# A hybrid decoder layer on one core: eight projections by seven products of quarter blocks, with sums of weight blocks on GpSimd

## The chip, the cores and the metric

The kernel runs on one NeuronCore of one Trainium2 chip, written directly against the engines: TensorE (PE) for products, VectorE (DVE), ScalarE (ACT) and GpSimd (POOL) for the rest, SyncE (SP) for most DMAs. Each engine works off its own list in order and waits on semaphores. The metric is the device time of one launch in microseconds (us). All data is float32.

## The reference

One layer on 256 tokens of width 2048 (batch 1). In short:

```
mod = silu(c) @ ada_w + ada_b                  # 2048 x 12288, split into six parts of 2048
h   = rms(x, g1) * (1 + sc1) + sh1
z   = h @ w_in                                 # 19 column groups of up to 512: m_*, b_*, r_*, n_*
y   = concat(mlstm(m_*), moba(b_*), retention(r_*), nsa(n_*))     # 4 heads of 128 each
x   = x + gate1 * (y @ w_out)
h2  = rms(x, g2) * (1 + sc2) + sh2
x   = x + gate2 * moe(h2)                      # 32 experts of width 512, top 2 of 8 in the top group
```

`nsa` also compresses its keys and values: windows of 32 tokens, flattened to 4096 values, go through a 4096x128 matrix (`cmp_w1`), GELU and a 128x128 matrix.

## The kernel before

**Layout.** The normalised tokens lie transposed in `hT` (128 partitions x 16 k-tiles x 256 tokens). The weights come as a stream of 88 "halves" of 2 MB (128 x 4096 floats, eight k-tiles of 512 columns) through a ring of four SBUF slots, `ring`, in the order of `STREAM`. SP issues the DMA of half i as soon as half i-4 has been used; who used it is known from `halves_used`. Two halves make a "chunk": the projection of one column group, called `chunk` in the code, 2048x512 weights.

**Stages.** (1) The start: eight steps that compute the first adaLN parts from halves shared by PE and DVE, and beside it three projections from rows that come by another path (`early`). (2) The list `ORDER`, which all engines walk through in step: chunks, steps of the four mixers, and `ada` steps. An `ada` step is 1/24 of the adaLN product, two halves, done wholly on DVE: a `tensor_scalar` and 15 `scalar_tensor_tensor` of 128x512, each adding weight tile times scalar to `ada_s`. PE then sums `ada_s` over partitions (`ada_combine`, the step `ada_sum`, right after the next chunk). (3) `y @ w_out` in four column blocks, with the router's products between. (4) The expert loop: 8 passes over 4 experts, 24 halves each, through eight slots of 2 MB, four of them ring slots.

**A chunk.** For a plain chunk PE multiplies each 128x128 tile of `hT` (stationary) with 512 columns of weights (moving): 32 matmuls into two PSUM banks of `W`, line 575. `m_q`, `m_k`, `r_q`, `r_k` are made transposed, 64 matmuls of 256 columns with weights stationary, line 567. ACT copies the result to SBUF in one instruction (line 1031). Consecutive chunks use different halves of `W`. DVE has nothing to do with a chunk. In a trace each float32 matmul stands as two records.

**Around it.** The compression (`cmp_hid`, line 636) runs 64 matmuls with a 128x128 weight tile stationary and 60 columns of windows moving. GpSimd takes square roots for norms (`rsqrt`, line 428, 128x8), issues a few DMAs, and clears a buffer before the experts (line 477); its list follows `ORDER` too. Sums of the g2 part of adaLN (`ada` steps 20 to 23) go through PE into `A`, and DVE adds them to `g2b`.

## Time and profile before

| | |
|---|---|
| median of 3 runs | 1763.21 us (1759.32 to 1765.27) |
| the profiled execution | 1761.94 us, its span 1759.4 us |
| busy | PE 1395.3 us (79%), PE weight loads 886.8 us, DVE 549.9 us, ACT 126.9 us, POOL 27.3 us |
| DMA | 613.18 MB, 349 GB/s on average |

The page of the profile gives for each engine its busy time; a line of 40 digits is the span in 40 slices of 44 us, busy share in tenths. Stage 1 ends at about 138 us, stage 2 at about 683 us, stage 3 at about 804 us, and the rest is the expert loop.

### The profile page before, as it was taken

The page shows a single profiled execution, that of the slowest core. Times are in us where ns is not written, and L with a number is a line of the kernel's source. Part 1 is how long each engine was busy: PE and PEld are TensorE (multiplying, and loading weights), DVE is VectorE, ACT ScalarE, POOL GpSimd, SP SyncE. Part 2 cuts the span into 40 slices and gives each one's busy share as a digit, 9 for nine tenths or more (in the row PEclk, how much of TensorE's full clock was granted, in tenths as well). Part 3 has the DMA queues.
Part 4 walks back from the last instruction along what each step waited for, and adds up shares of the span by engine and source line. Part 5 has one row for each costly group of instructions (what it writes and reads, how often), then busy time and mean ns, then how long its engine had stood idle before and what let it go on. Part 6 is the DMA issues. An engine that isn't in the chain of part 4 may idle for free.

```text
span 1759.4 us, 28215 instructions
## 1 busy us (share of the span) xinstructions
PE 1395.3 (79%) x12793; PEld 886.8 (50%) x12793; DVE 549.9 (31%) x902; ACT 126.9 (7%) x279; POOL 27.3 (2%) x30
## 2 busy tenths in 40 slices
PE   6998999999998998998677766776666666566757
PEld 4664755865444865467454443534443535344434
DVE  3545443754537343302212112121211120121203
ACT  2001010101000100002000000000000000000000
POOL 0000000000001000001000000000000000000000
PEclk9999799999999999998988788877887888788878
DMA  9997475766674584655999999999999999999995
GB/s 404 426 427 314 156 307 210 284 237 255 252 278 189 236 318 172 245 232 232 408 426 427 428 427 427 427 427 427 427 427 428 427 428 427 427 428 427 427 428 243
DMA packets 44615, 613.18 MB, mean 349 GB/s; under 512 B 4896, under 2 KB 5168, under 8 KB 6736
## 3 DMA queue, kind: packets, MB, share of 16 engines
q1 hardware_dynamic: 42848, 604.00, 83.0%
q0 software_dynamic: 1072, 6.44, 0.9%
q8 instruction: 109, 1.79, 0.4%
q10 hardware_dynamic: 576, 0.87, 0.1%
q14 instruction: 10, 0.08, 0.0%
HBM read 609.19 MB, written 2.10 MB: 347 GB/s over the span
## 4 chain that ended last, share of the span: by engine, by line
DMA 49%; PE 42%; DVE 6%; issue 1%; ACT 1%; POOL 0%; SPq 0%; DVEq 0%
DMA Zpad<-in_exp_w 34%; PE W L575 14%; DMA ring<-in_stream 8%; DMA ring<-in_exp_w 6%; PE M L939 5%; PE W L859 5%; PE W L567 3%; DVE ada_s L1230 3%; PE A L963 2%; PE W L913 2%; PE W L900 2%; PE W L841 2%; PE M L636 1%; PE M L551 1%; DVE tmp L1174 1%
## 5 line engine op out<-in xcount | busy, mean ns | idle before, releaser
L575 PE MATMUL W<-ring,buf_h 128*128 128x512 f32 x704 | 309.3, 600 | 4.2 <-DMA ring<-in_stream 4.1
L1230 DVE SCALAR_TENSOR_TENSOR ada_s<-ring,small,ada_s 128x512 f32<-128x512 f32 x296 | 222.6, 752 | 10.5
L575 PEld LDWEIGHTS W<-ring,buf_h 128*128 128x128 f32 x704 | 134.8, 193 | 171.6 <-issue 171.6
L939 PE MATMUL M<-ring,g1b 128*32 128x128 f32 x4096 | 153.5, 308 | 82.8 <-DMA ring<-in_exp_w 70.7
L939 PE MATMUL M<-Zpad,g1b 128*32 128x128 f32 x3072 | 129.1, 340 | 84.1 <-DMA Zpad<-in_exp_w 56.9
L939 PEld LDWEIGHTS M<-ring,g1b 128*32 128x32 f32 x4096 | 131.3, 124 | 115.8 <-DMA ring<-in_exp_w 93.8
L939 PEld LDWEIGHTS M<-Zpad,g1b 128*32 128x32 f32 x3072 | 113.1, 139 | 104.8 <-DMA Zpad<-in_exp_w 63.7
L1687 DVE SCALAR_TENSOR_TENSOR tmp<-tmp,M 128x128 f32<-128x128 f32 x32 | 9.2, 288 | 474.3 <-ACT tmp L1152 474.3
L1174 DVE TENSOR_TENSOR consts<-A,g2b 32x512 f32<-32x512 f32 x128 | 87.9, 687 | 213.7 <-PE A L963 210.7
L567 PE MATMUL W<-buf_h,ring 128*128 128x256 f32 x512 | 112.9, 383 | 11.1 <-DMA ring<-in_stream 11.1
L567 PEld LDWEIGHTS W<-buf_h,ring 128*128 128x128 f32 x512 | 98.1, 192 | 24.9 <-issue 11.5
L963 PE MATMUL A<-ring,tmp 128*32 128x512 f32 x512 | 80.0, 767 | 28.5 <-DMA ring<-in_exp_w 24.5
L963 PE MATMUL A<-Zpad,tmp 128*32 128x512 f32 x384 | 63.8, 795 | 37.5 <-DMA Zpad<-in_exp_w 34.3
L913 PE MATMUL W<-consts,tmp 128*128 128x512 f32 x128 | 72.0, 715 | 19.1 <-DVE buf_h L1174 19.1
L859 PE MATMUL W<-ring,buf_x 128*128 128x512 f32 x192 | 83.2, 593 | 1.2 <-ACT buf_x L1098 1.2
L900 PEld LDWEIGHTS W<-tmp,buf_x 128*128 128x128 f32 x576 | 70.2, 204 | 13.3 <-issue 13.2
L900 PE MATMUL W<-tmp,buf_x 128*128 128x128 f32 x576 | 71.9, 289 | 0.0
L1152 ACT ACTIVATE tmp<-M 128x128 f32<-128x128 f32 x32 | 8.9, 277 | 756.6 <-PE M L939 756.6
L1174 DVE TENSOR_TENSOR buf_h<-W,buf_h 128x2048 f32<-128x2048 f32 (+1 forms) x20 | 39.4, 1970 | 64.9 <-PE W L913 64.6
L541 PE MATMUL W<-buf_h,Zpad 128*128 128x256 f32 x256 | 58.3, 387 | 1.3 <-DVE buf_h L1255 1.3
L859 PEld LDWEIGHTS W<-ring,buf_x 128*128 128x128 f32 x192 | 36.2, 190 | 45.5 <-issue 44.0
L913 PEld LDWEIGHTS W<-consts,tmp 128*128 128x128 f32 x128 | 27.6, 226 | 58.6 <-issue 32.9
(285 smaller groups left out, 937.3 us busy)
## 6 DMA issues: line engine op xcount, KB each, us to landing
ring<-in_exp_w SPq DMA_DIRECT2D x96, 2048.0 KB, 35.6
ring<-in_stream SPq DMA_DIRECT2D x88, 2048.0 KB, 8.6
Zpad<-in_exp_w SPq DMA_DIRECT2D x72, 2048.0 KB, 36.6
PPY<-in_exp_w SPq DMA_DIRECT2D x24, 2048.0 KB, 35.5
Zpad<-in_early SPq DMA_DIRECT2D x8, 1536.0 KB, 10.6
buf_x<-in_x SPq DMA_DIRECT2D x2, 1024.0 KB, 6.7
buf_h<-in_x POOLq DMA_DIRECT2D x1, 2048.0 KB, 12.2
out<-buf_h SPq DMA_DIRECT2D x4, 512.0 KB, 3.1
```

Of the source, the lines that this page charges most:

```text
L541: ins = pe.matmul(dst[:, h * T:h * T + T], w[:, first + 512 * k + h * P:first + 512 * k + h * P + P], hT[:, kk, :], start=(kk == 0 and h % ...
L551: ins = pe.matmul(dst[:, tt * 512:tt * 512 + 512], hT[:, kk, tt * P:tt * P + P], w[:, first + 512 * k:first + 512 * k + 512], start=(kk == ...
L567: ins = pe.matmul(dst[:, h * T:h * T + T], w[:, 512 * k + h * P:512 * k + h * P + P], hT[:, kk, :], start=(kk == 0 and h % 2 == 0), stop=( ...
L575: ins = pe.matmul(dst[:, tt * 512:tt * 512 + 512], hT[:, kk, tt * P:tt * P + P], w[:, 512 * k:512 * k + 512], start=(kk == 0), stop=(kk == ...
L841: ins = pe.matmul(W[:, p0:p0 + 256], YT[:, kk, tt * P:tt * P + P], w[:, p1:p1 + 256], start=(kk == 0 and tt == 0), stop=(kk == KT - 1), sk ...
L859: ins = pe.matmul(W[:, o + tt * 512:o + tt * 512 + 512], YT[:, kk, tt * P:tt * P + P], w[:, 512 * k:512 * k + 512], start=(kk == 0), stop= ...
L900: ins = pe.matmul(W[:, k * P:k * P + P], xs[:, tt, k * P:k * P + P], tmp[:, 128 * tt:128 * tt + 128], start=(tt == 0), stop=(tt == 1))
L913: ins = pe.matmul(W[:, 512 * b:512 * b + 512], GT[:, tt * P:tt * P + P], ysb[:, 512 * b:512 * b + 512], start=True, stop=True)
L939: ins = pe.matmul(M[32 * c:32 * c + 32, 512 * w13:512 * w13 + 128], XT[:, kk, 32 * q:32 * q + 32], w[:, 512 * k + 128 * c:512 * k + 128 * ...
L963: ins = pe.matmul(A[32 * m:32 * m + 32, :], hTs[:, 32 * c:32 * c + 32], w[:, 2048 * c2 + 512 * m:2048 * c2 + 512 * m + 512], start=(c == 0 ...
L1174: return dve.tensor_tensor(o, x, y, op)
L1230: ins = dve.scalar_tensor_tensor(acc[:], w, cs[:, kk:kk + 1], acc[:], ALU.mult, ALU.add)
```

## The change

**Seven products.** For the eight chunks of `SEVEN`, weights and tokens are cut in quarters: `A11..A22` are 128-token by 8-k-tile quarters of `hT`, `B11, B12` the two column halves of the first weight half, `B21, B22` those of the second. Instead of eight quarter products there are seven, of sums and differences (the form of Strassen and Winograd). Each product is 8 matmuls of 256 columns into one bank of `W`; all four banks are used. DVE makes the four token sums `S1..S4` once, in `buf_x`. GpSimd makes four weight sums for each chunk, in place in the ring slots (`column_sums`), each a `tensor_tensor` of 128 x 2048. Two products are copied by ACT into the output, and DVE adds the rest in seven short operations (`add_quarters`), which stand in DVE's list where `ORDER` has the chunk, so behind the `ada` step ahead of it. Both halves of such a chunk are released only when the sixth or seventh product and all four weight sums are done.

**The rest.** The ring has five slots. In the last part of `ORDER` the `ada` steps 19 to 22 stand right behind their chunk. `cmp_hid` has the windows stationary (64 columns) and 128 weight columns moving, in two column groups of the array; a copy and two small matmuls then add the two groups. The four g2 `ada` steps accumulate in `g2b` itself; one set of four 512-column matmuls sums it over partitions while the router is worked out, and ACT copies it back. A few waits of the router's exponentials on DVE come later. The expert loop keeps its eight slots.

```diff
-         ('chunk', 'b_q'), ('m_pv', 0), ('norm', 'b_q'), ('ada', 19),
-         ('chunk', 'b_k'), ('turn', 'b_q'), ('turn_y', 'm'), ('norm', 'b_k'), ('ada', 20),
-         ('chunk', 'r_q'), ('turn', 'b_k'), ('scores', 'moba'), ('ada', 21),
-         ('chunk', 'r_k'), ('turn_p', 'moba'), ('ada', 22),
+         ('chunk', 'b_q'), ('ada', 19), ('m_pv', 0), ('norm', 'b_q'),
+         ('chunk', 'b_k'), ('ada', 20), ('turn', 'b_q'), ('turn_y', 'm'), ('norm', 'b_k'),
+         ('chunk', 'r_q'), ('ada', 21), ('turn', 'b_k'), ('scores', 'moba'),
+         ('chunk', 'r_k'), ('ada', 22), ('turn_p', 'moba'),
...
+                    of_kind, of_arg, of_hf = STREAM[i - RING]
                     if by_vector(STREAM[i - RING]):
                         sp.wait_ge(sem["ada_half_used"], dve_halves)
+                    elif of_kind == 'chunk' and of_arg in SEVEN:
+                        sp.wait_ge(sem["products_done"], 7 * SEVEN.index(of_arg) + 6 + of_hf)
+                        sp.wait_ge(sem["t_ready"], 4 * SEVEN.index(of_arg) + 4)
...
+            def column_sums(name):
+
+                n, _ = sevens(name)
+                (w0, full0, fills0), (w1, full1, fills1) = chunk_slots(name)
+                b11, b12, b21, b22 = side(w0, 0), side(w0, 1), side(w1, 0), side(w1, 1)
+                pool.wait_ge(full0, fills0)
+                pool.wait_ge(sem["products_done"], 7 * n + 1)
+                pool.tensor_tensor(b11, b12, b11, ALU.subtract).then_inc(sem["t_ready"], 1)
+                pool.wait_ge(sem["t_ready"], 4 * n + 1)
+                pool.wait_ge(full1, fills1)
+                pool.tensor_tensor(b12, b22, b12, ALU.subtract).then_inc(sem["t_ready"], 1)
+                pool.wait_ge(sem["products_done"], 7 * n + 3)
+                pool.wait_ge(sem["t_ready"], 4 * n + 2)
+                pool.tensor_tensor(b11, b22, b11, ALU.subtract).then_inc(sem["t_ready"], 1)
+                pool.wait_ge(sem["t_ready"], 4 * n + 3)
+                pool.tensor_tensor(b21, b21, b11, ALU.subtract).then_inc(sem["t_ready"], 1)
+
             for step, arg in ORDER:
-                if step == 'cmp_out':
+                if step == 'chunk' and arg in SEVEN:
...
+            def seven_products(name):
+
+                n, c = sevens(name)
+                (w0, full0, fills0), (w1, full1, fills1) = chunk_slots(name)
+                after_seven = CHUNKS[c - 1] in SEVEN
+
+                def product(i, left, w, col):
+                    b = i % 4 * 512
+                    for k in range(8):
+                        ins = pe.matmul(W[:, b:b + 256], left[:, k, :], w[:, 512 * k + 256 * col:512 * k + 256 * col + 256],
+                                        start=(k == 0), stop=(k == 7))
+                    ins.then_inc(sem["products_done"], 1)
+                    return ins
+
+                if after_seven:
+                    pe.wait_ge(sem["quarter_added"], 6 * n - 2)
+                else:
+                    pe.wait_ge(sem["chunk_copied"], 2 if n == 0 else c - 1)
+                pe.wait_ge(full0, fills0)
+                product(0, A11, w0, 0)
+                if after_seven:
+                    pe.wait_ge(sem["quarter_added"], 6 * n)
+                pe.wait_ge(full1, fills1)
+                product(1, A12, w1, 0)
+                pe.wait_ge(sem["t_ready"], 4 * n + 1)
+                if n == 0:
+                    pe.wait_ge(sem["s_ready"], 4)
+                else:
+                    pe.wait_ge(sem["chunk_copied"], c)
+                product(2, S1, w0, 0)
+                product(3, S4, w1, 1)
+                pe.wait_ge(sem["t_ready"], 4 * n + 2)
+                pe.wait_ge(sem["quarter_kept"], 2 * n + 1)
+                product(4, S3, w0, 1)
+                pe.wait_ge(sem["t_ready"], 4 * n + 3)
+                pe.wait_ge(sem["quarter_added"], 6 * n + 1)
+                product(5, S2, w0, 0)
+                pe.wait_ge(sem["t_ready"], 4 * n + 4)
+                pe.wait_ge(sem["quarter_kept"], 2 * n + 2)
+                product(6, A22, w1, 0)
+                half[0] += 2
...
                         pe.wait_ge(sem["blocks_ready"], w + 1)
                         for l in range(CMP_LEN):
-                            ins = pe.matmul(M[:, 512 * w:512 * w + 60], wt[:, l * P:l * P + P],
-                                            blk[w][:, l * 60:l * 60 + 60], start=(l == 0), stop=(l == CMP_LEN - 1))
+                            o = l % 2 * 64
+                            ins = pe.matmul(M[o:o + 64, 512 * w:512 * w + P], blk[w][:, l * 60:l * 60 + 64],
+                                            wt[:, l * P:l * P + P], start=(l < 2), stop=(l >= CMP_LEN - 2))
                         half_done(ins)
+                    pe.wait_ge(sem["hid_parts"], 1)
+                    for w in range(2):
+                        ins = pe.matmul(M[:, 1280 + 64 * w:1344 + 64 * w], hpart[:, w * P:w * P + P], const('selr'),
+                                        start=True, stop=True)
+                    ins.then_inc(sem["hid_summed"], 1)
...
+            def add_quarters(name):
+
+                n, c = sevens(name)
+                z = zslot[name]
+                z11, z12, z21, z22 = (z[:, 256 * i:256 * i + 256] for i in range(4))
+                right = z.rearrange("p (a h) -> p a h", a=TT)[:, :, 256:512]
+                second = z[:, 512:1024].rearrange("p (c h) -> p c h", c=2)
+
+                def twice(v):
+                    return v.unsqueeze(1).to_broadcast([P, 2, 256])
+
+                dve.wait_ge(sem["quarter_kept"], 2 * n + 1)
+                dve.wait_ge(sem["products_done"], 7 * n + 2)
+                tt_op(z11, W[:, 512:768], z21, ALU.add).then_inc(sem["quarter_added"], 1)
+                dve.wait_ge(sem["quarter_kept"], 2 * n + 2)
+                dve.wait_ge(sem["products_done"], 7 * n + 4)
+                tt_op(z12, W[:, 1536:1792], z22, ALU.add).then_inc(sem["quarter_added"], 1)
+                dve.wait_ge(sem["quarter_added"], 6 * n + 2)
+                tt_op(right, right, twice(z21), ALU.add).then_inc(sem["quarter_added"], 1)
+                dve.wait_ge(sem["quarter_added"], 6 * n + 3)
+                dve.wait_ge(sem["products_done"], 7 * n + 5)
+                tt_op(second, second, twice(W[:, 0:256]), ALU.add).then_inc(sem["quarter_added"], 1)
+                dve.wait_ge(sem["quarter_added"], 6 * n + 4)
+                dve.wait_ge(sem["products_done"], 7 * n + 6)
+                tt_op(z12, z12, W[:, 512:768], ALU.add).then_inc(sem["quarter_added"], 1)
+                tt_op(second, second, twice(W[:, 512:768]), ALU.add).then_inc(sem["quarter_added"], 1)
+                dve.wait_ge(sem["quarter_added"], 6 * n + 6)
+                dve.wait_ge(sem["products_done"], 7 * n + 7)
+                dve.wait_ge(sem["chunk_copied"], c)
+                tt_op(z21, z21, W[:, 1024:1280], ALU.add).then_inc(sem["chunk_copied"], 1)
+
```

On PE, in stage 2, the chunk `n_ks` stood before as two pieces, each waiting for its half (`slot_full`), followed by the sum of the `ada` step:

```order
L575 MATMUL W<-ring,buf_h 128x512 [waits slot_full2,chunk_copied]
L575 MATMUL W<-ring,buf_h 128x512 x15
L575 MATMUL W<-ring,buf_h 128x512 [waits slot_full3]
L575 MATMUL W<-ring,buf_h 128x512 x15
L532 MATMUL A<-consts,ada_s 128x1 [waits ada_combined,ada_half_used]
L532 MATMUL A<-consts,ada_s 128x1 x3
```

In the changed kernel the same place on PE reads (`t_ready` counts GpSimd's weight sums, `quarter_kept` ACT's copies, `quarter_added` DVE's additions):

```order
L610 MATMUL W<-ring,buf_h 128x256 [waits slot_full3,chunk_copied]
L610 MATMUL W<-ring,buf_h 128x256 x7
L610 MATMUL W<-ring,buf_h 128x256 [waits slot_full4]
L610 MATMUL W<-ring,buf_h 128x256 x7
L610 MATMUL W<-ring,buf_x 128x256 [waits s_ready,t_ready]
L610 MATMUL W<-ring,buf_x 128x256 x15
L610 MATMUL W<-ring,buf_x 128x256 [waits quarter_kept,t_ready]
L610 MATMUL W<-ring,buf_x 128x256 x7
L610 MATMUL W<-ring,buf_x 128x256 [waits quarter_added,t_ready]
L610 MATMUL W<-ring,buf_x 128x256 x7
L610 MATMUL W<-ring,buf_h 128x256 [waits quarter_kept,t_ready]
L610 MATMUL W<-ring,buf_h 128x256 x7
```

32 matmuls of 512 columns have become 56 of 256, and PE now waits inside the chunk for three other engines: the third product for the first weight sum, the sixth for DVE's first addition.

On GpSimd, the changed kernel's list around the chunks `n_vs` and `n_kw` is this (L454 is the square root, L475 to L483 the weight sums; before, only the three L454 rows, as L428, stood here):

```order
L454 TENSOR_TENSOR small<-small 128x8 [waits norm_ms]
L475 TENSOR_TENSOR ring<-ring 128x8x256 [waits products_done,slot_full4]
L478 TENSOR_TENSOR ring<-ring 128x8x256 [waits slot_full0,t_ready]
L481 TENSOR_TENSOR ring<-ring 128x8x256 [waits t_ready,products_done]
L483 TENSOR_TENSOR ring<-ring 128x8x256 [waits t_ready]
L454 TENSOR_TENSOR small<-small 60x1 [waits kc_ms]
L454 TENSOR_TENSOR small<-small 128x8 [waits norm_ms]
L475 TENSOR_TENSOR ring<-ring 128x8x256 [waits products_done,slot_full3]
L478 TENSOR_TENSOR ring<-ring 128x8x256 [waits slot_full4,t_ready]
L481 TENSOR_TENSOR ring<-ring 128x8x256 [waits t_ready,products_done]
L483 TENSOR_TENSOR ring<-ring 128x8x256 [waits t_ready]
```

So the weight sums of `n_vs` stand behind the square root of the norm of `n_q`, and those of `n_kw` behind that of `n_ks`.

On DVE, ahead of the additions of `m_v`, the changed kernel has the `ada` step 14 (L1345, L1347) and then the convolution of `m_k` (L1618 to L1629):

```order
L1345 TENSOR_SCALAR ada_s<-ring,small 128x512 [waits slot_full2,dve_step]
L1347 SCALAR_TENSOR_TENSOR ada_s<-ring,small,ada_s 128x512 [waits dve_step] x7
L1347 SCALAR_TENSOR_TENSOR ada_s<-ring,small,ada_s 128x512 [waits slot_full3,ada_half_used]
L1347 SCALAR_TENSOR_TENSOR ada_s<-ring,small,ada_s 128x512 [waits dve_step] x7
L1618 TENSOR_SCALAR Zpad<-Zpad,cols 128x256 [waits chunk_copied,ada_half_used]
L1618 TENSOR_SCALAR Zpad<-Zpad,cols 128x256 x3
...
L1293 TENSOR_SCALAR tmp<-tmp 128x1024 [waits conv_tanh]
L1629 SCALAR_TENSOR_TENSOR Zpad<-Zpad,tmp 128x1024 [waits dve_step]
L1286 TENSOR_TENSOR Zpad<-W,Zpad 128x256 [waits products_done,quarter_kept] x2
L1286 TENSOR_TENSOR Zpad<-Zpad 128x2x256 [waits quarter_added]
L1286 TENSOR_TENSOR Zpad<-Zpad,W 128x512 [waits products_done,quarter_added]
```

Before, the same work stood there without the last three rows; now the products of `m_v` past the fifth need it to be finished.

## Rows read from the trace of the kernel before

**Rows 1.** Stages: us, busy of PE, PEld, DVE, ACT, POOL, clock, DMA share, GB/s.

```profile
138.00:683.00 545.00, 516.19 (x1818) 320.53 (x1819) 264.97 (x401) 51.27 (x90) 13.85 (x12) 0.95 0.65 250
171.00:197.00 26.00, 25.66 (x129) 25.66 (x130) 4.22 (x12) 3.40 (x4) 0.00 (x0) 0.55 0.36 138
860.00:1740.00 880.00, 588.78 (x9307) 383.26 (x9296) 156.52 (x269) 39.59 (x126) 0.00 (x0) 0.82 1.00 424
```

**Rows 2.** Timeline of PE: start, us, instruction, idle before and its releaser.

```profile
138.31 29.40 PE L575 MATMUL W<-ring,buf_h 128*128 128x512 f32 x64 [3.75 <-DMA ring<-in_stream]
196.67 29.79 PE L575 MATMUL W<-ring,buf_h 128*128 128x512 f32 x64
...
230.55 27.70 PE L575 MATMUL W<-ring,buf_h 128*128 128x512 f32 x64
...
338.48 27.86 PE L567 MATMUL W<-buf_h,ring 128*128 128x256 f32 x128 [2.35 <-DMA ring<-in_stream]
...
369.75 27.63 PE L575 MATMUL W<-ring,buf_h 128*128 128x512 f32 x64
...
400.73 27.63 PE L575 MATMUL W<-ring,buf_h 128*128 128x512 f32 x64
...
573.10 29.47 PE L567 MATMUL W<-buf_h,ring 128*128 128x256 f32 x128 [8.71 <-DMA ring<-in_stream]
...
608.23 27.79 PE L567 MATMUL W<-buf_h,ring 128*128 128x256 f32 x128
...
770.51 1.08 PE L808 MATMUL A<-Zpad,consts 128*64 128x256 f32 x8
```

**Rows 3.** Page, costliest groups: busy us, mean ns of one.

```profile
L575 PE MATMUL W<-ring,buf_h 128*128 128x512 f32 x704 | 309.3, 600 | 4.2 <-DMA ring<-in_stream 4.1
```

**Rows 4.** Groups by line and shape: busy us, mean ns of one.

```profile
L1174 DVE TENSOR_TENSOR buf_h<-W,buf_h 128x2048 f32<-128x2048 f32 x16 | 36.7, 2291 | 64.6 <-PE W L913 64.6
...
L477 POOL MEMSET consts<- 32x2048 f32 x4 | 7.2, 1796 | 0.7 <-PE M L817 0.4
```

**Rows 5.** Timeline of POOL.

```profile
201.81 1.67 POOL L428 TENSOR_TENSOR small<-small 128x8 f32<-128x8 f32 x1 [78.02 <-DVE small L1177]
...
233.38 1.65 POOL L428 TENSOR_TENSOR small<-small 128x8 f32<-128x8 f32 x1 [2.98 <-DVE small L1177]
...
537.58 2.03 POOL L428 TENSOR_TENSOR small<-small 128x8 f32<-128x8 f32 x1 [135.81 <-DVE small L1177]
...
687.08 2.03 POOL L428 TENSOR_TENSOR small<-small 128x8 f32<-128x8 f32 x1 [11.56 <-DVE small L1177]
...
806.02 7.54 POOL L477 MEMSET consts<- 32x2048 f32 x4 [0.39 <-PE M L817]
```

**Rows 6.** Timeline of DVE in stage 2, with the `ada` steps 9 and 15.

```profile
204.66 0.48 DVE L1228 TENSOR_SCALAR ada_s<-ring,small 128x512 f32<-128x512 f32 x1
205.18 11.78 DVE L1230 SCALAR_TENSOR_TENSOR ada_s<-ring,small,ada_s 128x512 f32<-128x512 f32 x15
...
384.87 1.14 DVE L1454 TENSOR_SCALAR Zpad<-Zpad,cols 128x256 f32<-128x256 f32 x4
...
392.99 1.23 DVE L1465 SCALAR_TENSOR_TENSOR Zpad<-Zpad,tmp 128x1024 f32<-128x1024 f32 x1
...
405.42 11.78 DVE L1230 SCALAR_TENSOR_TENSOR ada_s<-ring,small,ada_s 128x512 f32<-128x512 f32 x15
```

**Rows 7.** Timeline of DVE beside three of POOL's pieces of rows 5.

```profile
537.39 0.69 DVE L1181 TENSOR_SCALAR Zpad<-Zpad 128x1024 f32<-128x1024 f32 x1
...
687.62 1.22 DVE L1174 TENSOR_TENSOR PPY<-PPY,Zpad 128x1024 f32<-128x1024 f32 x1
...
812.67 0.92 DVE L1626 TENSOR_SCALAR small<-small 128x8 f32<-128x8 f32 x1
```

**Rows 8.** Timeline of PE: a sum of an `ada` step; the wait in the router.

```profile
602.41 1.02 PE L529 MATMUL A<-ada_s,consts 128*128 128x512 f32 x2
...
810.90 0.69 PE L888 MATMUL M<-tmp,consts 128*128 128x64 f32 x2 [5.04 <-DVE tmp L1174]
```

More of the change, by code:

```diff
@@ L101 @@
 MIXED = 'nmbr'
+SEVEN = ('n_ks', 'n_vs', 'n_kw', 'n_vw', 'm_v', 'm_o', 'b_v', 'r_v')
 MIX_Y = {'m': 0, 'b': 1, 'r': 2, 'n': 3}
@@ L125 @@
 STREAM = weight_stream()
-RING = 4
+RING = 5
 HALF = 8 * 512
@@ L139, in halves_used @@
     v = sum(by_vector(STREAM[j]) for j in range(i))
-    return i - v, v
-FIRST_FILLS = EXPERT_BASE // RING
+    seven = sum(STREAM[j][0] == 'chunk' and STREAM[j][1] in SEVEN for j in range(i))
+    return i - v - seven, v
+FIRST_FILLS = [len(range(i, EXPERT_BASE, RING)) for i in range(RING)]
 EXPERT_RING = 8
@@ L608, in _ @@
                     ada_combine(arg)
+                elif step == 'chunk' and arg in SEVEN:
+                    seven_products(arg)
                 elif step == 'chunk':
@@ L1284, in _ @@
             for step, arg in ORDER:
-                if step == 'ada':
+                if step == 'chunk' and arg in SEVEN:
+                    add_quarters(arg)
+                elif step == 'ada':
                     ada_accumulate(arg)
```

186 lines of the change are left out of this document (118 added, 68 removed).

## The prediction

> **What bounds the kernel now.** I read the stages first. In the expert loop the DMA engines are busy all the time at 424 GB/s while PE is busy for 589 of 880 us; in stage 2 PE is busy for 516 of 545 us and the DMA engines for 65% of it [rows 1]. So from 138 to about 804 us PE's list sets the pace, and after that the transfers, whose number does not change. A microsecond taken out of PE's path ahead of the experts starts that train of transfers a microsecond earlier, and so comes off the end; one taken out of PE in the loop would be worth nothing. Everything below is therefore a sum over PE's time in stages 2 and 3.
>
> Then PE's timeline. A chunk takes 27.6 us (the row at 400.73); the first takes 29.4, the one behind the compression 29.8, both with an idle or slow stretch just ahead of them [rows 2]. Over its 11 chunks the line is busy for 309.3 us [rows 3], 28.1 each, so the eight that change cost 225 us. The compression fills the stretch from 171 to 197 us, at a mean granted clock of 0.55, near the lower level of 1.2 GHz, although PE is busy for 25.7 of 26 us in it [rows 1]. Three more places matter: waits of 2.35 and 8.71 us for ring halves, the second followed by a chunk of 29.5 us where its like takes 27.8 [rows 2].
>
> **The change, part by part.** *Products.* 64 matmuls of 256 columns take 27.79 us [rows 2], so a product of 8 takes p = 3.47 us. Seven take 24.3 us against 27.6, if PE never waits. But it does wait. The first weight sum can start when product 1 is done, at 3.47 us, and product 3 needs it. With s for one sum, product 3 starts at 3.47 + s, and five products follow: the chunk takes 20.8 + s by this path, and 6.9 + 4s by GpSimd's own chain, which the last product closes.
>
> *What s is.* The trace has no such operation on GpSimd. Its one pass over 2048 elements, a memset, takes 1.80 us [rows 4]; a sum makes two reads and a write. If these ran wholly beside each other, s would be 1.8 us; one after another, 5.4 us. DVE's nearest operation takes 2.29 us [rows 4]. GpSimd is a programmed engine (a square root of 8 elements takes 1.67 us [rows 5]), so I take the upper part: two and a half passes, 4.5 us. Then the chunk takes 25.3 us, 2.3 less than before. The bounds give 24.3 (s under 3.47) and 28.5 us. The Trainium skill (GPSIMD Engine Reference, "Performance versus the Vector engine") gives 4497 ns for such a float32 sum and says to leave elementwise work to the Vector engine; by it the chunk would come out at the same 25.3 us. No run shows it yet.
>
> *Where GpSimd comes late.* In its list the sums of `n_vs` stand behind the square root of the norm of `n_q`, which ended 6.8 us into that chunk (201.81 + 1.67 - 196.67), those of `n_kw` behind one that ended 4.5 us into theirs (233.38 + 1.65 - 230.55) [rows 2, 5]. These chunks become 6.8 + 4.5 + 5 x 3.47 = 28.7 and 26.3 us.
>
> *Where DVE comes late.* Product 6 needs DVE's first addition, and that stands behind an `ada` step. If DVE is free for it D us after the chunk's start, the chunk takes at least D + 0.45 + 2p = D + 7.4. From the trace of before D is 20.3 for `n_vs` (216.96 - 196.67), 16.3 for `m_o` (417.2 - 400.9) and 24.5 for `m_v`, with the convolution between (394.22 - 369.75) [rows 2, 6]; the other five lie between 12.7 and 18.0 and end in the same way. Only `m_v` is bound by it: 31.9 us. Sums so far: 27.6 for the first chunk (25.3, and 2 us as before for its start and for the second half, which lands 2.1 MB / 424 GB/s = 4.9 us after the first and is now needed at 3.5), 28.7, 26.3, 31.9 and four of 25.3: 215.7 us, 10 less than before.
>
> *What the two engines do to each other.* The trace shows one thing surely. A tiny `TENSOR_SCALAR` on DVE, of 8 elements, lasted 0.92 us and ended at 813.59, just when GpSimd's memsets ended (806.02 + 7.54 = 813.56) [rows 5, 7]. And a square root on GpSimd took 2.03 us instead of 1.67 both times that it began during a `TENSOR_SCALAR` of 1024 elements on DVE [rows 5, 7]. So one-input operations of DVE from and to SBUF and any GpSimd operation exclude each other, for the whole operation. Each `ada` step begins with one (0.48 us), and the convolution has four [rows 6]. Where it falls within a sum of up to 4.5 us, DVE is late by the rest: in `n_vs` by 3.3 us (8.0 against 11.3), in `n_kw` by 3.3, in `m_o` by 4.0 (4.0 against 8.0), in `m_v` by about 6 (from 15, through two sums). By D + 7.4 these become 31.0, 28.7, 27.7 and 38 us. The eight chunks then come to 229 us, 4 **more** than before: in my forecast the seven products save nothing.
>
> *Compression.* The nearest row to 64 stationary and 128 moving columns in two groups is line 808: 4 matmuls (8 records) of 256 columns in 1.08 us, with 64 [rows 2]. Half as wide, 64 matmuls take 64 x 0.13 = 8.3 us. A copy of 0.4 us, two small matmuls and the hops between add 1.2. Against 25.7 us that is **-16**; if the clock stays at its lower level, 17 + 1.2 us, so -7.5. I take the first, as wide matmuls ran at the upper level just ahead.
>
> *Ring and order.* With `ada` 19 behind chunk `b_q` DVE does it while it now idles, and half i waits for i-5: the waits of 8.71 and 2.35 us go, and 1.7 of slow start: **-12.8**. Nothing else is late next: a chunk's first half waits for an `ada` half that DVE drops at D, 10 us before the next chunk, and lands in about 5.
>
> *g2.* Four sums of 0.86 us leave PE's path; the four matmuls that take their place lie in a wait of 5.04 us [rows 8], and ACT's copy of 2 us ends about when the gather starts: **-3.2**. DVE's four token sums of 1024 elements, some 5 us, lie where it waits for PE at the end of stage 1. The memsets, semaphores and late exponentials cost nothing, as they lie beside PE's work; uncovered they would be under 1 us.
>
> Sum: 4 - 16 - 12.8 - 3.2 = **-28 us**. The profiled execution took 1761.9 us (span 1759.4), 1.3 under the median. 1761.9 - 28 = **1734 us**.
>
> **The rivals.** *B: the engines hardly touch each other.* Then the chunks give their 10 us: -10 - 32 = -42, so 1720 us. For it: the exclusion is shown only for one-input operations. With s at its lower bound the chunks could lose another 10: 1710.
>
> *C: operations with two SBUF inputs are excluded too* (all 15 `scalar_tensor_tensor` of an `ada` step). Then DVE and GpSimd take turns, one operation each: while four sums of 4.5 us run, DVE gets about four of its 0.75 us steps. D grows by 18, and every chunk becomes D + 25.4: from 38 to 50 us, 341 us for the eight, 116 more than before: 1761.9 + 116 - 32 = 1846 us. It decides from 4 us more in each chunk, where it eats up the other 32. For it: both would read through what the shorter ones fight for. Against it: the `TENSOR_TENSOR` at 687.62 had two inputs in SBUF, ran while GpSimd's square root ran (687.08 to 689.11), took its usual 1.22 us, and did not lengthen that one beyond 2.03 [rows 5, 7]; but that operation reads only 8 elements. The Trainium skill says so outright (SBUF — State Buffer, "SBUF: two separate sides"): DVE in a two-port mode, or with two SBUF inputs against a GpSimd operation that reads SBUF, and GpSimd hold an exclusive lock for the whole instruction. By that rule the result is C; the rows bear it out for the first kind only. If DVE keeps the lock until its `ada` step is through, the sums start at D instead, and it ends near 1800.
>
> *D: a wash.* s at 5.4 us or a partial exclusion puts 3 to 4 us more on each chunk, and gains and losses cancel: 1755 to 1770.
>
> **How the numbers follow.** Forecast (1722 to 1750): 0.38. B: 0.22. C: 0.32, as the mechanism is half shown. D: 0.08. Faster by over 0.3%: the first two and a quarter of D, 0.62. Within 0.3%, about what a measurement can tell here, half of D: 0.04. Slower: C and the rest, 0.34. The range from 1708 to 1846 leaves out the far half of C and little else; the forecast's own is 1720 to 1750.
>
> **What would show it.** The weight sums on GpSimd at 4.5 us; PE waiting in the sixth product of `n_vs`, `n_kw`, `m_o` and above all `m_v` for DVE; `TENSOR_SCALAR` of `ada` steps stretched to some us, but `SCALAR_TENSOR_TENSOR` at 0.75; the compression under 10 us with the clock above 0.9; no wait for the ring ahead of `r_q`; the expert loop as long as before. I would be wrong if `SCALAR_TENSOR_TENSOR` rows stretch beside GpSimd's sums or have gaps of their length (C), if the sums take over 5.5 us, if the compression runs at 1.2 GHz, or if halves of the ring, released late by chunks that hold both, make PE wait anew.

## The result, and the profile after

The changed kernel takes 1850.47 us (median of 4 runs, 1849.3 to 1851.36), the kernel before 1762.1 us in the same comparison (1759.32 to 1765.27). The ratio is 1.0501, with a 95% interval of 1.048 to 1.0521: 88 us slower, where I had forecast 28 us less, and 4.5 us outside my range. What happened is rival C, at 1846 us. The profiled execution has a span of 1849.2 us. Two of the kernels below had one execution each in a slower state, 1949 and 1964 us at a granted clock of 0.72 instead of 0.90; these two stand in the medians given, which they move by under 0.5 us, and in no ratio.

The stages first, with the columns of [rows 1]: all of stage 2, which now ends where the first product of `y @ w_out` starts, at 774.7 us; in it the compression; and the same piece of the expert loop, counted back from the end.

```profile
138.00:774.70 636.70, 487.90 (x2200) 385.19 (x2201) 426.25 (x456) 48.59 (x98) 166.83 (x44) 0.89 0.56 218
184.30:192.60 8.30, 7.71 (x133) 7.47 (x133) 4.29 (x12) 3.40 (x4) 0.00 (x0) 1.00 0.98 374
949.80:1829.80 880.00, 574.71 (x9288) 375.59 (x9280) 156.45 (x269) 39.56 (x126) 0.00 (x0) 0.84 1.00 423
```

The expert loop is what it was, at 423 GB/s with the DMA engines always busy. The compression is short and at the full clock, as forecast. The rest of stage 2 is another place: PE was busy for 516 of 545 us, now for 488 of 637, while DVE went up from 265 to 426 us and GpSimd from 14 to 167. PE does less and waits. For what, the list of PE's waits says (total us, times, longest):

```profile
PE W L610 <- DVE Zpad L1286: 92.0, 7, 15.7
...
PE W L610 <- ACT Zpad L1133: 23.7, 1, 23.7
```

Line 610 is the loop of the seven products. Seven of the eight chunks wait for DVE's additions, and `m_v` for a copy by ACT. The page's groups of DVE name the reason:

```profile
L1347 DVE SCALAR_TENSOR_TENSOR ada_s<-ring,small,ada_s 128x512 f32<-128x512 f32 x236 | 289.0, 1225 | 8.4
```

These 236 operations take 1225 ns on average, where the form took 752 before. Some of them lie in stage 1. The groups by line and shape from 138 to 810 us tell them apart from the others:

```profile
L1347 DVE SCALAR_TENSOR_TENSOR ada_s<-ring,small,ada_s 128x512 f32<-128x512 f32 x180 | 246.9, 1372 | 6.4
...
L1347 DVE SCALAR_TENSOR_TENSOR g2b<-ring,small,g2b 128x512 f32<-128x512 f32 x52 | 39.1, 751 | 1.7
L1286 DVE TENSOR_TENSOR Zpad<-Zpad,small 128x1024 f32<-128x1024 f32 x5 | 14.7, 2941 | 8.8 <-POOL small L454 8.8
L1345 DVE TENSOR_SCALAR ada_s<-ring,small 128x512 f32<-128x512 f32 x12 | 14.3, 1189 | 0.1
```

The steps into `g2b`, late in the stage, where no weight sum runs beside them, are at 751 ns; those into `ada_s`, 12 steps of which 8 stand beside sums, at a mean of 1372.

GpSimd's sums themselves are of the length that I took, 4.5 us alone. One chunk in full, `n_kw`, from the timelines of POOL, DVE and PE (start, us, instruction, idle before and its releaser):

```profile
247.45 4.49 POOL L475 TENSOR_TENSOR ring<-ring 128x2048 f32<-128x2048 f32 x1
252.02 5.38 POOL L478 TENSOR_TENSOR ring<-ring 128x2048 f32<-128x2048 f32 x1
257.55 4.51 POOL L481 TENSOR_TENSOR ring<-ring 128x2048 f32<-128x2048 f32 x1
262.14 4.82 POOL L483 TENSOR_TENSOR ring<-ring 128x2048 f32<-128x2048 f32 x1
```

```profile
247.51 5.52 DVE L1286 TENSOR_TENSOR Zpad<-Zpad,small 128x1024 f32<-128x1024 f32 x1 [1.76 <-POOL small L454]
252.95 4.74 DVE L1345 TENSOR_SCALAR ada_s<-ring,small 128x512 f32<-128x512 f32 x1
257.72 20.02 DVE L1347 SCALAR_TENSOR_TENSOR ada_s<-ring,small,ada_s 128x512 f32<-128x512 f32 x15
277.78 0.75 DVE L1286 TENSOR_TENSOR Zpad<-W,Zpad 128x256 f32<-128x256 f32 x2
```

```profile
242.70 7.07 PE L610 MATMUL W<-ring,buf_h 128*128 128x256 f32 x32
252.00 10.63 PE L610 MATMUL W<-ring,buf_x 128*128 128x256 f32 x48 [2.23 <-POOL ring L475]
278.35 6.75 PE L610 MATMUL W<-ring,buf_x 128*128 128x256 f32 x16 [15.73 <-DVE Zpad L1286]
284.94 3.62 PE L610 MATMUL W<-ring,buf_h 128*128 128x256 f32 x16
```

Read it across. A multiplication with two SBUF inputs, 1.22 us when alone, is issued 0.06 us behind the first sum and lasts 5.52 us: it waited until that sum was over, at 251.94, and ran. The second sum needed 0.9 us more than the first and the third, because it waited for that multiplication in turn. The `tensor_scalar` then sat out the second sum. The 15 steps of the `ada` took 20.02 instead of 11.78 us, 8.2 more, while two sums took 9.3: DVE got one operation in between each two sums and no more. PE has products 1 to 5 done at 262.63, 15.2 us before DVE comes to its first addition at 277.78.

Where only `scalar_tensor_tensor` stands beside all four sums, in the next chunk `n_vw`, the picture is purest (timelines of DVE, then POOL's first and last sum):

```profile
295.37 28.44 DVE L1347 SCALAR_TENSOR_TENSOR ada_s<-ring,small,ada_s 128x512 f32<-128x512 f32 x15
```

```profile
300.08 4.50 POOL L475 TENSOR_TENSOR ring<-ring 128x2048 f32<-128x2048 f32 x1 [33.12 <-PE W L610]
...
314.50 4.82 POOL L483 TENSOR_TENSOR ring<-ring 128x2048 f32<-128x2048 f32 x1
```

28.44 us instead of 11.78 is 16.7 more, and the four sums cover 19.2 us (300.08 to 319.32). The difference, 2.6 us, is about three steps of 0.75: the three operations let through between four sums. One step by itself, the one that begins while the second sum runs:

```profile
305.16 4.89 DVE L1347 SCALAR_TENSOR_TENSOR ada_s<-ring,small,ada_s 128x512 f32<-128x512 f32 x1
```

Its neighbours begin at 300.10, 310.08 and 315.00: one step for each sum, as long as the sum. From the second sum on each lasts 0.3 us longer than the 4.50 of the first; my reading is that it waits for the step that was let through.

So each chunk of seven products costs about D + 25.4 us, as rival C had it (D is where DVE was free before, from the start of the chunk, read from the timelines of the kernel before). The eight, from PE's timeline, start of the first product to the end of the last, against that formula:

| chunk | n_ks | n_vs | n_kw | n_vw | m_v | m_o | b_v | r_v | sum |
|---|---|---|---|---|---|---|---|---|---|
| D + 25.4 | 41.1 | 45.7 | 43.3 | 38.3 | 49.9 | 41.9 | 40.7 | 40.6 | 341 |
| measured | 41.7 | 46.3 | 45.9 | 39.3 | 52.5 | 42.1 | 41.1 | 41.2 | 350 |

The formula comes this close by two errors that offset each other. In the seven chunks other than `m_v` DVE reached its first addition 0.9 to 1.6 us earlier than D + 18, as three of its steps got through between the sums. And the last two products, for which it has 6.9 us, took 8.6 to 10.2, at granted clocks of 0.70 to 0.83 behind PE's wait of 9 to 16 us, 15 us over the seven chunks. In `n_kw`:

```profile
278.35:288.56 10.21, 10.21 (x35) 8.49 (x35) 2.58 (x5) 0.00 (x0) 0.00 (x0) 0.70 0.79 279
```

Against 226 us before the eight cost 124 us more, by the two timelines; the spans of the two profiled executions differ by 90; so all the rest of the change gave back about 34 us.

### The profile page after: what moved, and what is told of

Read it like the earlier page. It is cut to its first block, busy times and chain, and to the rows that moved or that the text cites. A ratio compares the mean times of both kernels' runs of the same rounds, so it can differ in the third digit from the quotient of the medians.

```text
span 1849.2 us, 29213 instructions
## 1 busy us (share of the span) xinstructions
PE 1354.3 (73%) x13181; PEld 942.2 (51%) x13181; DVE 715.4 (39%) x961; ACT 126.1 (7%) x288; POOL 180.3 (10%) x62
## 4 chain that ended last, share of the span: by engine, by line
DMA 44%; PE 36%; DVE 13%; issue 3%; POOL 1%; ACT 1%; SPq 0%; DVEq 0%; POOLq 0%
DMA Zpad<-in_exp_w 40%; DVE ada_s L1347 9%; PE W L657 6%; PE W L957 4%; PE W L665 4%; PE W L610 4%; PE M L1040 3%; PE W L587 2%; DMA ring<-in_exp_w 2%; PE A L1064 2%; PE W L939 2%; DMA ring<-in_stream 2%; PE M L597 1%; PE W L1013 1%; PE W L1000 1%
## 5 line engine op out<-in xcount | busy, mean ns | idle before, releaser
L1347 DVE SCALAR_TENSOR_TENSOR ada_s<-ring,small,ada_s 128x512 f32<-128x512 f32 x236 | 289.0, 1225 | 8.4
L1040 PE MATMUL M<-ring,g1b 128*32 128x128 f32 x4096 | 165.8, 329 | 102.5 <-DMA ring<-in_exp_w 97.3
L610 PE MATMUL W<-ring,buf_x 128*128 128x256 f32 x512 | 130.4, 419 | 128.7 <-DVE Zpad L1286 92.0
L1040 PEld LDWEIGHTS M<-ring,g1b 128*32 128x32 f32 x4096 | 143.7, 134 | 134.1 <-DMA ring<-in_exp_w 118.2
L610 PEld LDWEIGHTS W<-ring,buf_x 128*128 128x128 f32 x512 | 107.3, 213 | 151.7 <-issue 118.7
L1040 PE MATMUL M<-Zpad,g1b 128*32 128x128 f32 x3072 | 115.0, 306 | 73.1 <-DMA Zpad<-in_exp_w 41.3
L1040 PEld LDWEIGHTS M<-Zpad,g1b 128*32 128x32 f32 x3072 | 98.6, 123 | 95.2 <-DMA Zpad<-in_exp_w 47.6
L610 PE MATMUL W<-ring,buf_h 128*128 128x256 f32 x384 | 90.8, 394 | 5.3 <-DMA ring<-in_stream 5.3
L610 PEld LDWEIGHTS W<-ring,buf_h 128*128 128x128 f32 x384 | 75.6, 199 | 17.5 <-issue 5.6
L665 PE MATMUL W<-ring,buf_h 128*128 128x512 f32 x192 | 83.0, 593 | 0.0
```

The source lines that it names most:

```text
L610: ins = pe.matmul(W[:, b:b + 256], left[:, k, :], w[:, 512 * k + 256 * col:512 * k + 256 * col + 256], start=(k == 0), stop=(k == 7))
L665: ins = pe.matmul(dst[:, tt * 512:tt * 512 + 512], hT[:, kk, tt * P:tt * P + P], w[:, 512 * k:512 * k + 512], start=(kk == 0), stop=(kk == ...
L1040: ins = pe.matmul(M[32 * c:32 * c + 32, 512 * w13:512 * w13 + 128], XT[:, kk, 32 * q:32 * q + 32], w[:, 512 * k + 128 * c:512 * k + 128 * ...
L1347: ins = dve.scalar_tensor_tensor(acc, w, cs[:, kk:kk + 1], acc, ALU.mult, ALU.add)
```

## The experiments

The theory: a GpSimd operation that reads SBUF and a DVE operation with two inputs in SBUF exclude each other for whole instructions and take turns; the eight chunks are slow through that alone, and the rest of the change gains some 32 us. The rivals are named with each.

### Without seven products

All eight chunks in the plain form; ring, order, compression and g2 as changed. ACT's tanh of `m_o`, which stood with the seven products' copies, stands behind the plain copy.

```diff
-SEVEN = ('n_ks', 'n_vs', 'n_kw', 'n_vw', 'm_v', 'm_o', 'b_v', 'r_v')
+SEVEN = ()
```

> The changed kernel with no chunk done by seven products: all chunks as before (28 us each), the five ring slots, the order, the compression and the g2 sums as changed. Theory 1 (everything lost is lost in the eight chunks, by DVE and GpSimd taking turns): the other parts give their 32 us and a little more, as the compression's 64 matmuls took 7.4 us in the changed kernel's trace: 1728 us, 122 under the changed kernel. Rival (the five slots or the order themselves hurt, by transfers that come late): 1745 or more.

Measured: 1730.37 us, ratio 0.9792 (0.976 to 0.9825), and in a later comparison once more:

> The kernel without seven products again, on the same chip as old_ring_and_order: 1730 us, 2% under the kernel before.

Measured: 1731.57 us, ratio 0.98 (0.9773 to 0.9827). Here PE never waits for a chunk's weights but once, for 3.8 us, at the start of stage 2. The rest of the change is worth 33 us in this comparison and 30 in the later one, against the 32 of my sum, and this version beats both kernels. The eight seven-product chunks cost 120 us.

### What on GpSimd does the harm

Memsets in place of the weight sums, of the same total length: GpSimd is as busy and signals after about the same time, but reads nothing from SBUF.

```diff
-                pool.tensor_tensor(b11, b12, b11, ALU.subtract).then_inc(sem["t_ready"], 1)
+                fill(b11).then_inc(sem["t_ready"], 1)     # 2 memsets of 1.8 us, one of 0.95
... (the other three sums in the same way)
```

(The count of the expert rounds is set to one in this run and the next.)

> GpSimd's four sums of a chunk are replaced by memsets of the same region with about the same length (two of 1.8 us and one of 0.9, which read nothing); the weights of products 3 to 7 are thus constants, and the number of expert rounds is fixed at the one it has. Theory 1a (the exclusion is over the interface through which GpSimd and DVE's second input read): DVE's 15 additions of an ada step run at 0.75 us beside the memsets, only its one-input operations wait, at most 1.8 us: 1715 to 1735 us. Theory 1b (any GpSimd operation stops them): about 1850 us. Rival 2 (GpSimd's chain of four sums is what holds PE, not DVE): the chain is as long as before, so 1850 us too.

Measured: 1740.15 us, ratio 0.9871 (0.9855 to 0.9888). The groups of DVE and POOL by shape, stage 2:

```profile
L1356 DVE SCALAR_TENSOR_TENSOR ada_s<-ring,small,ada_s 128x512 f32<-128x512 f32 x180 | 135.3, 752 | 6.4
L1354 DVE TENSOR_SCALAR ada_s<-ring,small 128x512 f32<-128x512 f32 x12 | 7.7, 642 | 0.1
L1295 DVE TENSOR_TENSOR Zpad<-Zpad,small 128x1024 f32<-128x1024 f32 x5 | 6.1, 1224 | 8.8 <-POOL small L454 8.8
```

```profile
L473 POOL MEMSET ring<- 128x2048 f32 x64 | 116.1, 1814 | 126.4 <-PE W L619 122.9
```

With GpSimd busy as before but writing only, both two-input forms are back at 752 and 1224 ns. The one-input `TENSOR_SCALAR` is not: 642 ns, where it takes 480 with GpSimd idle. Those two classes of exclusion are thus told apart. It also refutes the rival by which GpSimd's chain of four holds PE whatever DVE does, at 1850 us. The upper end of the expectation, 1735, was 5 us too low: PE still waits 13.6 us for GpSimd and 12.9 once, in `m_v`, for ACT:

```profile
PE W L619 <- POOL ring L475: 13.6, 11, 3.1
PE W L619 <- ACT Zpad L1142: 12.9, 1, 12.9
```

So even where the engines hardly touch, the seven products cost 10 us over the kernel without them. Chunk by chunk on PE's timelines that is `m_v` alone: it takes 42.0 us, where the plain one takes 27.6; the other seven come to 197 us against 198. My rival B, 1720 us by a gain of 10 in the chunks, does not come out either, as it had `m_v` at 31.9.

### Which inputs on DVE do the harm

The weight sums as changed, but the `scalar_tensor_tensor` of the `ada` steps 8 to 17 reads its addend from PSUM (`A`), so that it has one input in SBUF.

```diff
-    ins = dve.scalar_tensor_tensor(acc, w, cs[:, kk:kk + 1], acc, ALU.mult, ALU.add)
+    ins = dve.scalar_tensor_tensor(acc, w, cs[:, kk:kk + 1],
+                                   A[:] if N_PAIRED <= n < 18 else acc, ALU.mult, ALU.add)
```

> GpSimd's sums stay. In the ada steps 8 to 17 the 15 additions read their addend from the PSUM tile A instead of SBUF, so they have one input in SBUF (their result is not the adaLN product then; the number of expert rounds is fixed at the one it has). Theory 1 (two SBUF inputs are what collides): the additions run beside the sums at 0.7 to 0.75 us; what still collides is the first operation of each step and the norms' products with two inputs, once in four chunks: 1730 to 1745 us. Rival (any DVE operation that reads SBUF is stopped, whatever its inputs): about 1850 us.

Measured: 1759.66 us, ratio 0.9977 (0.9965 to 0.9989). Groups of DVE and POOL by shape, stage 2:

```profile
L1347 DVE SCALAR_TENSOR_TENSOR ada_s<-ring,small,A 128x512 f32<-128x512 f32 x150 | 112.2, 748 | 5.3
L1286 DVE TENSOR_TENSOR Zpad<-Zpad,small 128x1024 f32<-128x1024 f32 x5 | 14.7, 2942 | 8.8 <-POOL small L454 8.8
L1345 DVE TENSOR_SCALAR ada_s<-ring,small 128x512 f32<-128x512 f32 x12 | 14.2, 1188 | 0.1
```

```profile
L475 POOL TENSOR_TENSOR ring<-ring 128x2048 f32<-128x2048 f32 x8 | 36.1, 4518 | 133.9 <-PE W L610 133.9
```

Beside the same sums the same operation takes 748 ns when one of its inputs comes from PSUM, and the first of the four sums takes 4.52 us on average. Nothing is left of the mutual wait but in the forms that this run did not touch: the norm's multiplication (2942 ns, with two inputs in SBUF) and the one-input `TENSOR_SCALAR` (1188 ns). They hold DVE up enough that PE still waits for it, 15.5 us in three chunks, and 13.9 in `m_v`. 91 of the 120 us are gone. The time is 15 us above the range that I expected, as I had named those forms and counted them too low, and had not counted `m_v`'s wait for ACT.

### DVE's first addition earlier

The first addition between the two halves of the `ada` step, in all chunks but `m_v`, so that product 6 does not wait for its second half.

```diff
+                ada_rows(n, 0, ...)
+                if n in after:
+                    add_first(after[n])
+                ada_rows(n, 1, ...)
```

> A correct kernel: DVE's first addition of a chunk, for which product 6 waits, stands between the two halves of the ada step instead of behind it (not in m_v, which has another step between). Theory 1 (turns of 4.5 us and 0.75 us): PE no longer waits in the chunk, but DVE's list is as long as before, 12 us of ada step and 18 us of GpSimd's sums one after another, and the next chunk's first product waits for DVE's fourth addition: 5 us less in seven chunks, about 1815 us. Rival (only the place of the addition in DVE's list was wrong): PE's wait of 9 to 16 us goes wholly, about 1750 us or less.

Measured: 1806.58 us, ratio 1.0243 (1.0226 to 1.026). PE's wait for DVE falls from 92.0 us to 32.9. A little over a third of the loss is gone, 44 of 120 us; the rest stays, as DVE loses as much in each chunk wherever the addition stands (the mean of its `ada_s` steps is 1389 ns), `m_v` still waits 23.7 us for ACT, and the waits for halves of the ring go up from 5.3 to 12.3 us.

### The same seven products with and without DVE's work beside them

Three chunks only, `m_o`, `b_v`, `r_v`; then the same with the `ada` steps 15, 16, 17 moved behind `r_v`, which shifts 18 and 19 too; then that move alone. (With plain chunks ahead of them, PE's first product in the two kernels with three waits for the copy of the chunk just ahead, not of the one before it.)

```diff
-SEVEN = ('n_ks', 'n_vs', 'n_kw', 'n_vw', 'm_v', 'm_o', 'b_v', 'r_v')
+SEVEN = ('m_o', 'b_v', 'r_v')
# the move
-         ('chunk', 'm_v'), ('scores', 'win'), ('ada', 15),
-         ('chunk', 'm_o'), ('turn_p', 'win'), ('pv', 'win'), ('ada', 16),
-         ('chunk', 'b_v'), ('m_decay', 0), ('ada', 17),
-         ('chunk', 'r_v'), ('turn_y', 'n'), ('m_scores', 0), ('ada', 18),
-         ('chunk', 'b_q'), ('ada', 19), ('m_pv', 0), ('norm', 'b_q'),
-         ('chunk', 'b_k'), ('ada', 20), ('turn', 'b_q'), ('turn_y', 'm'), ('norm', 'b_k'),
+         ('chunk', 'm_v'), ('scores', 'win'),
+         ('chunk', 'm_o'), ('turn_p', 'win'), ('pv', 'win'),
+         ('chunk', 'b_v'), ('m_decay', 0),
+         ('chunk', 'r_v'), ('turn_y', 'n'), ('m_scores', 0), ('ada', 15), ('ada', 16),
+         ('chunk', 'b_q'), ('ada', 17), ('m_pv', 0), ('norm', 'b_q'), ('ada', 18),
+         ('chunk', 'b_k'), ('ada', 19), ('turn', 'b_q'), ('turn_y', 'm'), ('norm', 'b_k'), ('ada', 20),
```

> The changed kernel with seven products in m_o, b_v and r_v only; the other five chunks take the plain form. Theory (turns): the DVE work that stands ahead of the first addition in these three (ada 15, 16, 17) is slowed by the four sums as in the changed kernel, where the three chunks took about 42, 41 and 41 us against 27.7: some 40 us over the kernel without seven products (1730), so about 1770 us, and SCALAR_TENSOR_TENSOR in these three ada steps at a mean of over 1.2 us, in the others at 0.75. Rival (the seven products cost by themselves, by hops and late halves of the ring, whatever DVE does beside them): also slower than 1730, but then by the same amount when the ada steps are moved away (the run three_sevens_ada_later).

> The same three chunks with seven products, but the ada steps 15, 16, 17 moved behind r_v, so that DVE has only short softmax and decay work beside the sums, and its first addition comes in time. Theory (turns): the loss of about 40 us goes nearly all; b_v and r_v come to 25 to 27 us each, m_o to about 28, and the kernel to 1725 to 1735 us, if moving the steps costs nothing by itself (see ada_later_alone). Rival (the form costs by itself): about 1770 us, as in three_sevens_beside_ada.

> No seven products, ada steps 15, 16, 17 behind r_v: what the move costs by itself. DVE was busy for 166 us of the 404 between 400 and 804 us in the kernel before, so there is room: 1730 us give or take 4, the same as the kernel without seven products. If the halves of the moved steps crowd the ring or the norms of b_q and b_k come late, up to 1750.

Measured: 1768.76 us (ratio 1.0024, 1.0002 to 1.0046), 1756.16 us (0.9951, 0.9928 to 0.9974), and 1758.44 us for the move alone (0.9954, 0.9932 to 0.9977). The first is on its expectation: 38 us over the kernel without seven products, 12.8 for each chunk. PE's timeline shows `b_v` in it, and behind it `b_v` in the second:

```profile
428.27 7.07 PE L610 MATMUL W<-ring,buf_h 128*128 128x256 f32 x32
436.95 10.63 PE L610 MATMUL W<-ring,buf_x 128*128 128x256 f32 x48 [1.61 <-POOL ring L475]
460.67 5.60 PE L610 MATMUL W<-ring,buf_x 128*128 128x256 f32 x16 [13.09 <-DVE Zpad L1285]
466.11 3.62 PE L610 MATMUL W<-ring,buf_h 128*128 128x256 f32 x16
```

```profile
414.52 7.07 PE L610 MATMUL W<-ring,buf_h 128*128 128x256 f32 x32
422.85 14.08 PE L610 MATMUL W<-ring,buf_x 128*128 128x256 f32 x64 [1.25 <-POOL ring L475]
437.01 3.72 PE L610 MATMUL W<-ring,buf_h 128*128 128x256 f32 x16
```

41.5 us (428.27 to 469.73) against 26.2 (414.52 to 440.73), with the same four sums on GpSimd in both. In the second, PE waits 3.8 us in all three chunks together, for GpSimd, and never for DVE. That refutes the rival by which the form costs by itself. It also shows what the form is worth at its best here: 1.4 us in `b_v`, where a plain chunk takes 27.6; `r_v`, at a lower clock for its first products, takes 28.0. Even there DVE's own two-input addition meets a sum (timeline of DVE, second kernel; 0.69 us alone):

```profile
430.58 2.00 DVE L1285 TENSOR_TENSOR Zpad<-Zpad 128x512 f32<-128x512 f32 x1
```

I was wrong on the move, which I had at 1730 us give or take 4. It costs 28 us by itself, and the list of PE's waits of that kernel says where:

```profile
PE W L665 <- DMA ring<-in_stream: 13.6, 3, 7.0
PE W L657 <- DMA ring<-in_stream: 9.9, 1, 9.9
```

DVE had the time, but halves are loaded in the stream's order, and those of the moved steps crowd where they now stand; my reading is that they hold the ring's slots until DVE, with two steps in a row, has used them. So the second kernel is to be compared with the third, not with 1730: it is 2 us faster, with ranges that overlap (1753.55 to 1759.15 us and 1750.88 to 1761.82 us). With DVE out of the way, seven products neither gain nor lose what can be measured.

### The other terms

The compression as before, and in the second comparison the ring and the order of the last part, each alone and both, all without seven products.

```diff
# old_compression
-   ins = pe.matmul(M[o:o + 64, 512 * w:512 * w + P], blk[w][:, l * 60:l * 60 + 64],
-                   wt[:, l * P:l * P + P], start=(l < 2), stop=(l >= CMP_LEN - 2))
+   ins = pe.matmul(M[:, 512 * w:512 * w + 60], wt[:, l * P:l * P + P],
+                   blk[w][:, l * 60:l * 60 + 60], start=(l == 0), stop=(l == CMP_LEN - 1))
# four_ring_slots, old_ring_and_order
-RING = 5
+RING = 4
# old_order, old_ring_and_order
-         ('chunk', 'b_q'), ('ada', 19), ('m_pv', 0), ('norm', 'b_q'),
+         ('chunk', 'b_q'), ('m_pv', 0), ('norm', 'b_q'), ('ada', 19),
...
```

> No seven products, and the compression as in the kernel before (weights stationary, 60 moving columns). By my sum the compression was worth 16 us with 1.2 of hops inside, by the two profiles 25.6 against 8.2 us, 17.4: 1746 to 1748 us. If the granted clock in that stretch was not the compression's doing, less: about 1738.

Measured: 1748.46 us, ratio 0.9909 (0.9879 to 0.9939): 18 us more than without it. PE's timeline in this kernel, and behind it in the one without seven products:

```profile
172.94 12.07 PE L728 MATMUL M<-Zpad,ring 128*128 128x60 f32 x64 [1.33 <-DVE PPY L1455]
184.81 13.86 PE L728 MATMUL M<-tmp,ring 128*128 128x60 f32 x64
198.46 29.60 PE L665 MATMUL W<-ring,buf_h 128*128 128x512 f32 x64
```

```profile
172.04 3.71 PE L729 MATMUL M<-ring,Zpad 128*64 128x128 f32 x64 [1.33 <-DVE PPY L1461]
175.59 3.66 PE L729 MATMUL M<-ring,tmp 128*64 128x128 f32 x64
179.78 0.66 PE L734 MATMUL M<-consts,PPY 128*128 128x64 f32 x4 [0.53 <-DVE PPY L1501]
180.27 27.69 PE L665 MATMUL W<-ring,buf_h 128*128 128x512 f32 x64
```

From the first product to the next chunk it is 25.5 us (172.94 to 198.46) against 8.2 (172.04 to 180.27), 17.3 apart, and that chunk takes 29.6 instead of 27.7. The window over the compression in the first of the two, columns as in [rows 1]:

```profile
172.90:198.40 25.50, 25.46 (x128) 25.46 (x129) 3.86 (x10) 3.40 (x4) 0.00 (x0) 0.54 0.34 133
```

PE is busy for all of it, at a mean granted clock of 0.54, close to the lower level of 1.2 GHz. The kernels differ in nothing but the compression; in the other one the stretch from 155 to 200 us, with the new form in it, ran at 1.00. So the fall of the clock is the old form's doing. Scaled by the clock, its 25.5 us would be 13.8 at the upper level: by this estimate, 11.7 of the 17.3 us are the clock and the rest the shorter work.

> No seven products, ring of 4 slots as in the kernel before, new order of the last part. The waits of 8.71 and 2.35 us were both ascribed to the ring and the order together, 12.8 us. If the fifth slot carries it, the kernel goes back to about 1742 us; if the order alone does (DVE frees the ada half in time), it stays at 1730 to 1733.

> No seven products, five slots, the old order of the last part (ada 19 behind the norm of b_q). If the fifth slot is enough by itself, 1730 to 1733 us; if the wait of 8.71 us ahead of r_q needs the order, 1739 us.

> No seven products, four ring slots and the old order of the last part together. One alone cost 6 (slots) and 4 us (order) over the kernel without seven products. If the term of 12.8 us in the prediction is right, both together cost 12 to 13: about 1743 us. If the two simply add, 1740.

Measured: 1736.29 us (0.985, 0.9829 to 0.9871), 1734.73 us (0.9839, 0.9818 to 0.986) and 1748.23 us (0.992, 0.9907 to 0.9934), against 1731.57 us with both changes, measured beside the last of them. By the medians the old slots alone cost 5 us and the old order alone 3, both together 17. The five executions of the kernel without seven products spread from 1720.83 to 1734.16 us, so only the 17 is clear of the noise. The traces settle what the medians leave open: beyond the 3.8 us at the start of stage 2, PE waits 4.3 us for ring halves with the old slots, 3.3 with the old order and 14.2 with both. So either of the two takes most of the wait away, and the second adds little. In the kernel with both undone the wait ahead of `r_q` is there again, with the slower chunk behind it:

```profile
560.18 29.89 PE L657 MATMUL W<-buf_h,ring 128*128 128x256 f32 x128 [8.24 <-DMA ring<-in_stream]
```

## Why the prediction was wrong

**The step that failed** is "What the two engines do to each other". It took the exclusion for one-input operations of DVE only and left `scalar_tensor_tensor` at 0.75 us; beside a sum of 4.5 us it takes 4.9, and so the eight chunks took 350 us where the sum had 229. I had the rule on the table as rival C, with the right mechanism (turns, one operation each) and nearly the right time, and gave it 0.32. That its 341 us for the eight chunks come within 3% is in part luck, by the two offsetting errors above. The Trainium skill (SBUF — State Buffer, "SBUF: two separate sides") says that an operation of DVE with two SBUF inputs and a GpSimd operation that reads SBUF hold the shared ports by an exclusive lock for the whole instruction. The traces here agree in each part: two inputs in SBUF and sums, 4.9 us for the step beside a sum and 1372 ns on average over the stage; one of them from PSUM, 748; GpSimd writing only, 752.

**Why I weighed it wrongly.** My evidence against was one row, the `TENSOR_TENSOR` at 687.62 beside a square root [rows 5, 7]. It began 0.54 us into GpSimd's instruction of 8 elements, and took its usual 1.22 us. I noted that this instruction reads only 8 elements, and still let the row weigh more than that. Beside an instruction that reads 2048 elements for 4.5 us the same form took 5.52. Why the short one let it through, and what it holds for how long, no run here isolates.

**The terms of the sum:**

- *s, 4.5 us:* right, 4.49 to 4.51 us when DVE was not in between.
- *A chunk of 25.3 us when nothing collides:* nearly. `b_v` took 26.2 us in the run with DVE's steps away; product 3 starts at 8.33 us, where I had 7.97, and the five products from there take 17.9 us instead of 17.35.
- *Eight chunks, 229 us:* 350 measured. Rival C's 341 was 9 us short. In `n_kw` (2.5 us more than the formula) that is the clock after the wait: DVE was there 0.9 us early, and the last two products took 10.2 us. (D of `m_o`, 16.3 in the prediction, is 16.5 by the row at 400.73.) In `m_v` (2.6 us more) the stretched `ada` step delays the convolution, and with it ACT's tanh, behind which ACT's copy of the first product stands in its list. The fifth product waits for that copy, so that PE has three products left when it goes on, where I had counted two behind DVE's addition. I had not followed that edge; it is also what the memset run's 10 us are.
- *Compression, -16:* right, a little low. 18 measured.
- *Ring and order, -12.8:* 17 measured, with the spread said above. The mechanism is right; with both undone, PE waits 18.0 us for the ring, of which 3.8 stays anyway. The 14.2 left are more than the 11.4 of the kernel before.
- *g2, -3.2:* not measured alone. The kernel without seven products is 31 us faster than before, while compression, ring and order account for 35. So g2 and all that I took at nothing come to about +4 together instead of -3, though the spread of that kernel is as large. By the profiles of before and of the kernel without seven products, stage 2 starts 0.7 us later (138.31 and 139.02), it is 31.9 shorter, the piece from there to the first expert product 2.2 shorter (140.1 and 137.9), and the rest 1.8 longer (936.4 and 938.3). What holds up the last stays open.
- *What an earlier microsecond is worth:* right. Stage 2 took 91 us more (138.31 to 682.84, now 139.09 to 774.70), and the span grew by 90.

**The rivals.** B (the engines hardly touch) fell by the result, and its gain did not come in the run with memsets either: the seven products cost 10 us there. The products from the third on hang on GpSimd's sums, the fifth and the last also on ACT and the sixth on DVE; those waits, 14.4 us of loss in `m_v` first of all, and the stretched one-input forms cost more than the 26 us that the eight chunks save by one product less (8 x 3.3). D did not occur.

## What to carry to other kernels

Before work is put on an idle GpSimd, list DVE's operations that will stand beside it by the number of inputs that they read from SBUF: here each with two waited out a whole GpSimd sum of 4.5 us, and so the offload was paid on DVE's list at nearly its full length (16.7 of 19.2 us). If DVE's list is what the bound engine waits for, the offload is lost; what helps is an operand in PSUM, or the two at different times. A row is evidence against contention only for instructions like those in it: the one that I leaned on had 8 elements on GpSimd's side, and the sums have 2048.

And fewer products are not less time where each now hangs on two other engines: the best chunk measured here gained 1.4 us of 27.6, and those of the changed kernel lost 11 to 25.
